# Gated attention's head norm: from TensorE sums and a ScalarE root to a GpSimd reduction and power

## What is computed

```python
y = xf * lax.rsqrt(jnp.mean(xf * xf, axis=-1, keepdims=True) + NORM_EPS)
return (y * g).astype(x.dtype)
```

## Time and profile before

| | |
|---|---|
| median of 3 runs | 1993.37 us (1993.0 to 1993.6) |
| the profiled execution | 1993.1 us, of which the span is 1991.3 us |
| granted TensorE clock | 0.999 of full speed |
| busy share of the span | PE 99%, PEld 83%, DVE 51%, ACT 35%, POOL 20% |
| dense tiles of this layer end, softmax steps begin | at about 152 us of the span |
| last transpose of the softmax steps | at 240.4 us |

### The profile page before, as it was taken

One profiled execution on the slowest core, in us unless ns is written; L12 is line 12 of the kernel. 1 busy time (PEld: TensorE's weight loads), 2 busy tenths in 40 slices (PEclk: granted clock), 3 DMA queues, 4 the chain that ended last, 5 costly groups with the idle time before them and its releaser, 6 DMA issues.

```text
span 1991.3 us, 27158 instructions
## 1 busy us (share of the span) xinstructions
PE 1975.5 (99%) x11044; PEld 1656.8 (83%) x11044; DVE 1019.7 (51%) x1391; ACT 694.5 (35%) x1008; POOL 404.9 (20%) x212
## 2 busy tenths in 40 slices
PE   9999999999999999999999999999999999999998
PEld 7878888888888888889888888888877888888887
DVE  5468758357345336626727535642543664322435
ACT  6357643122124323315312212534434252222222
POOL 1000007686600101000669661000000200000000
PEclk9999999999999999999999999999999999999999
DMA  6221134444333232232445442232221223323231
GB/s 198 74 61 44 46 114 159 157 139 153 123 104 117 84 97 85 85 113 89 148 140 167 148 146 87 85 106 76 70 80 64 86 84 106 102 99 106 84 106 64
DMA packets 135032, 208.91 MB, mean 105 GB/s; under 512 B 6346, under 2 KB 105864, under 8 KB 134920
## 3 DMA queue, kind: packets, MB, share of 16 engines
q1 hardware_dynamic: 125952, 180.37, 28.0%
q0 software_dynamic: 6912, 25.17, 3.8%
q10 hardware_dynamic: 2056, 1.76, 0.3%
HBM read 205.18 MB, written 2.10 MB: 104 GB/s over the span
## 4 chain that ended last, share of the span: by engine, by line
PE 94%; DVE 3%; ACT 2%; issue 0%; POOL 0%; ACTq 0%; POOLq 0%
PE ps L2149 28%; PE ps L2151 28%; PE ps L2150 28%; PE ps L2210 1%; PE ps L2600 1%; PE ps L2203 1%; PE ps L2202 1%; PE ps L2611 1%; PE ps L2700 1%; PE ps L2173 1%; PE ps L2792 1%; PE ps L2155 0%; DVE m L1460 0%; PE ps L2589 0%; PE ps L2588 0%
## 5 line engine op out<-in xcount | busy, mean ns | idle before, releaser
L1382 DVE TENSOR_TENSOR w_lo<-w_raw,w_hi 128x2048 fp32r<-128x2048 f32 x149 | 349.9, 2349 | 569.2 <-ACT w_hi L726 569.2
L2149 PE MATMUL ps<-x_hi,w_hi 128*128 128x512 f32 x1240 | 487.8, 393 | 0.4 <-DVE w_lo L1382 0.4
L2151 PE MATMUL ps<-x_hi,w_lo 128*128 128x512 f32 x1240 | 482.9, 389 | 0.0
L2150 PE MATMUL ps<-x_lo,w_hi 128*128 128x512 f32 x1240 | 482.8, 389 | 0.0
L726 ACT ACTIVATE w_hi<-w_raw 128x2048 fp32r<-128x2048 f32 x151 | 288.9, 1913 | 536.0 <-PE ps L2151 434.9
L2149 PEld LDWEIGHTS ps<-x_hi,w_hi 128*128 128x128 f32 x1240 | 233.3, 188 | 50.0 <-issue 2.5
L2151 PEld LDWEIGHTS ps<-x_hi,w_lo 128*128 128x128 f32 x1240 | 232.8, 188 | 49.1
L2150 PEld LDWEIGHTS ps<-x_lo,w_hi 128*128 128x128 f32 x1240 | 233.0, 188 | 46.3
L2149 PE MATMUL ps<-w_hi,h_hi 128*128 128x512 f32 x688 | 267.8, 389 | 0.0
L2151 PE MATMUL ps<-w_hi,h_lo 128*128 128x512 f32 x688 | 267.7, 389 | 0.0
L2150 PE MATMUL ps<-w_lo,h_hi 128*128 128x512 f32 x688 | 267.6, 389 | 0.0
(11 more groups left out here) (404 smaller groups left out, 2695.5 us busy)
## 6 DMA issues: line engine op xcount, KB each, us to landing
w_raw<-in_ffn_w SPq DMA_DIRECT2D x64, 1024.0 KB, 5.4
ada_w<-in_w_ada POOLq DMA_DIRECT2D x48, 512.0 KB, 4.1
w_raw<-in_w_ffn_in SPq DMA_DIRECT2D x22, 1024.0 KB, 5.1
w_raw<-in_w_in SPq DMA_DIRECT2D x20, 1024.0 KB, 5.4
w_raw<-in_o_w_in SPq DMA_DIRECT2D x16, 1024.0 KB, 5.4
w_raw<-in_w_ffn_out SPq DMA_DIRECT2D x11, 1024.0 KB, 4.9
w_raw<-in_e_w_in SPq DMA_DIRECT2D x9, 1024.0 KB, 5.4
w_raw<-in_o_w_out SPq DMA_DIRECT2D x8, 1024.0 KB, 4.8
```

Source lines behind the costliest of these rows:

```text
L1382: nc.vector.tensor_tensor(w_lo[:, slot, :], w_raw[:, slot, :], w_hi[:, slot, :].bitcast(F32), ALU.subtract).then_inc(w_lo_ready, 1)
L2149: nc.tensor.matmul(dst, a_hi, b_hi, start=start, stop=False)
L2150: nc.tensor.matmul(dst, a_hi, b_lo, start=False, stop=False)
L2151: return nc.tensor.matmul(dst, a_lo, b_hi, start=False, stop=stop_)
```

## The change

The sum over partitions is made by GpSimd with one `partition_all_reduce` over all four heads (128x2048), which leaves the sum on all partitions. GpSimd then scales it and adds the epsilon (TENSOR_SCALAR) and raises it to -0.5 (TENSOR_TENSOR with the operation pow) for each head. VectorE multiplies these into `o_gla` inside the softmax steps, at u = 3, 6, 8 and 10. The TensorE sums and spreads, ScalarE's root and VectorE's reciprocal go. The first copy of `n_prob_t` waits for the reduction, since it overwrites the squares. Two waits of TensorE on `gn_done` go with the PSUM banks that they protected.

```diff
+        gn_root = place("gn_root", [P, 4, SEQ], Y_ + 44)
...
+            pool.wait_ge(gn_sq, 1)
+            chain.link(nc.gpsimd.partition_all_reduce(gn_root[:, :, :].rearrange("p h t -> p (h t)"),
+                                                      gn_square[:, :, :].rearrange("p h t -> p (h t)"), P,
+                                                      bass.bass_isa.ReduceOp.add))
+            pool.sem_inc(gn_summed, 1)
+            for hd in range(GLA_HEADS):
+                part = gn_root[:, hd, :]
+                chain.link(nc.gpsimd.tensor_scalar(part, part, 4.0 / P, 4.0 * EPS, ALU.mult, ALU.add))
+                nc.gpsimd.tensor_tensor(part, part, neg_half[:, 0:1].broadcast_to([P, SEQ]), ALU.pow).then_inc(gn_rooted, 1)
...
-                if x == 18:
-                    act.wait_ge(gn_mm, 1)
-                    nc.scalar.activation(gn_sum[:, :], ps[:, 4, :], ACT.Sqrt, scale=4.0 / P,
-                                         bias=small[:, 21:22]).then_inc(gn_ms, 1)
...
             take_r(DENSE_E)
+            act.wait_ge(gn_summed, 1)
             for u in range(N_N):
...
             def gn_scale(hd):
-                dve.wait_ge(gn_spread, hd + 1)
-                nc.vector.scalar_tensor_tensor(o_gla[:, hd, :], o_gla[:, hd, :], gla_norm[:, hd:hd + 1], ps[:, 3 + hd, :],
+                dve.wait_ge(gn_rooted, hd + 1)
+                nc.vector.scalar_tensor_tensor(o_gla[:, hd, :], o_gla[:, hd, :], gla_norm[:, hd:hd + 1], gn_root[:, hd, :],
                                                ALU.mult, ALU.mult).then_inc(gn_done, 1)
...
-                    dve.wait_ge(gn_ms, 1)
-                    nc.vector.reciprocal(gn_sum[:, :], gn_sum[:, :]).then_inc(gn_rs, 1)
-                if x == 19:
-                    for hd in range(GLA_HEADS):
-                        gn_scale(hd)
...
+                if u in (3, 6, 8, 10):
+                    gn_scale((3, 6, 8, 10).index(u))
...
-                if x == 17:
-                    gn_sums()
...
-                if x == 19:
-                    gn_spreads()
...
                 if u >= 2:
                     pe.wait_ge(n_exped, 2 * u - 2)
-                elif u:
-                    pe.wait_ge(gn_done, 1)
-                else:
+                elif u == 0:
                     pe.wait_ge(bank_free, 4 + DENSE_E)
...
                 if u:
                     pe.wait_ge(n_copied, 2 * (u - 1) + z + 1)
-                else:
-                    pe.wait_ge(gn_done, 2 + 2 * z)
```

More of the change, by code:

```diff
@@ L304, in program @@
             "gla_a", "gla_am", "gla_ket", "gla_ds", "gla_s", "gla_o", "gla_oe"))
-        gn_sq, gn_mm, gn_ms, gn_rs, gn_spread, gn_done = (sem(x) for x in (
-            "gn_sq", "gn_mm", "gn_ms", "gn_rs", "gn_spread", "gn_done"))
+        gn_sq, gn_summed, gn_rooted, gn_done = (sem(x) for x in ("gn_sq", "gn_summed", "gn_rooted", "gn_done"))
         cmp_multiplied, cmp_copied = sem("cmp_multiplied"), sem("cmp_copied")
@@ L2525, in o_gla_of @@
                 o.then_inc(gla_o, 1)
[L2527 to L2538, removed]
             def in_the_middle(x):
```

## The result

The changed kernel takes 2299.2 us (median of 4 runs, 2298.33 to 2299.49) against 1993.4 us: the ratio is 1.153, 95% interval 1.1521 to 1.1548. The change costs 305.8 us. The range on record ended at 2033 us.

What follows compares the result with a forecast made beforehand. TensorE, 94% of the chain, was taken as the bound. Terms: -2.1 (matmuls) + 0.9 (reduction) + 11.9 (shared ports) + 1.4 (products) = +12.1 us on 1993.1, with 0.3 to the median 2005.5 us; range 1991 to 2033 us.

Steps and rivals of the forecast that it cites:

- The size of the power: GpSimd's power on 128x512, in no row: taken as 2.7 times a 1.4 us scaling, 4 us per head.
- The place of the loss: Forecast in the softmax steps: VectorE's scalings held at the shared ports while GpSimd runs its powers, +11.9 us.
- the rival of the slow routine: Powers beyond 7 us a head make GpSimd bound the first softmax steps: about 2015 us upward, chance 0.20.
- VectorE idle ahead of the new products: Sign in the softmax steps that the roots are late, and the ports not the cause; no size given.
- I assume that a long power holds the ports throughout: Softmax steps: each 4 us power blocks VectorE's scalings, so a step takes 6.3 us instead of 2.5.
- the +11.9 us: Softmax steps: port stalls beside GpSimd's scaling and power pairs, +0.5 for the first and +11.4 for the other three.
- The row of 1.67 us: Earlier one-column GpSimd power beside a long VectorE scaling: 1.67 instead of 0.60 us, ending 0.43 us after VectorE's.
- The reduction: GpSimd's sum beside VectorE's compressed attention chain: 12.3 us long, four instructions held 0.9 us each, +0.9 us.
- the rows at 454.00: VectorE beside an earlier reduction: a two-SBUF-tile instruction took 1.57 for 0.69 us, the cast behind it 1.29 for 0.43.
- What went: TensorE's sums and spreads of the old norm, 1.00 + 1.07 us: -2.1 us, the most the change can bring.
- the covered reciprocal: VectorE's reciprocal in the old norm, 3.35 us, hidden beside TensorE's other work; its removal counted at nothing.
- The late reduction: Rival: the reduction ends past 159.2 us and holds ScalarE's copies, 1.5 us at 24.5 us length; chance 0.03.

Runs made afterwards that it cites:

- without powers: The changed kernel with GpSimd's four powers left out, the root missing from the output: 2001.5 us, ratio 1.0041 to the kernel before.
- the moved reduction: The changed kernel with its four powers left out and the reduction started only after weight tile 10's low part: 1993.75 us, ratio 1.0004 to the kernel before.

## Why the prediction was wrong

**The size of the power** is the step that failed: "I take the ratio of the two one-column rows, 0.60 / 0.22 = 2.7, as that of the running part too". It measured 81.97 us where the step had 4, twenty times as much. The bounds held (1.28 and 195 us), but the choice between them did not rest on a row: the surplus of 0.38 us on one column was taken for start-up, and 0.16 of it was the price of the column. The row that is nearest in kind, the power itself, bounded from above and was the better guide; the product of the same shape shares only the shape. The range stopped at 12 us and left 0.12 beyond it, too little for a cost with two ends a factor 150 apart.

**The place of the loss** was named only in the rival of the slow routine: VectorE waits for the roots, the scalings stand behind it, TensorE behind these. Its arithmetic holds with the measured size: 155.8 + 4 x (1.4 + 82) puts the fourth root at 489.4 us, and its power ended at 489.0 (a start 0.6 us later and slightly shorter pairs nearly cancel). One of the prediction's own signs of being wrong, VectorE idle ahead of the new products, is what the profile shows. The memset of `v_cmp` is a point that all kernels share. Its line in GpSimd's timeline and the transposes of the steps, changed kernel first, then without powers:

```profile
92.98 0.53 POOL L645 MEMSET v_cmp<- 128x512 f32 x1 [75.13 <-PE ps L2431]
...
L2583 PEld LDWEIGHTS ps<-ident,n_prob x160: 137/141/231, 167.8 to 546.7; 128*128 128x128 f32 x160
```

```profile
93.95 0.53 POOL L645 MEMSET v_cmp<- 128x512 f32 x1 [75.16 <-PE ps L2431]
...
L2583 PEld LDWEIGHTS ps<-ident,n_prob x160: 137/140/143, 169.1 to 249.4; 128*128 128x128 f32 x160
```

Before, the memset is at 92.15 us and the transposes at 160.6 to 240.2. Counted from the memset to the last transpose, the changed kernel is 305.7 us longer: 6.4 us until the first transpose (7.2 of stall, less 2.1 of matmuls, and a remainder of 1.3, where the clock is low behind the stall), 0.7 us that the steps cost also without powers, 292.2 us of waits for the roots, and 6.4 us more in the steps (378.9 - 80.3 - 292.2). In that last part TensorE runs at the lower clock behind each wait, and two pairs of VectorE's scalings meet GpSimd's next scaling (1.70 us for 0.87, 1.82 for 1.00). It is a remainder, not an experiment.

**"I assume that a long power holds the ports throughout"** was wrong, and it was the whole mechanism of the +11.9 us. Powers leave the ports to VectorE in the changed kernel and beside the kernel before. The row of 1.67 us showed a power waiting for VectorE, which says nothing about the reverse.

**The reduction** was sized rightly in itself (12.3 us forecast, 11.89 measured) and wrongly in what it does to others: +0.9 us where 7.2 came, 8.5 with the remainder that goes with the clock. The step took 0.9 us per instruction from the rows at 454.00, which began 2.6 us before that reduction's end; in the changed kernel the product came 1.1 us after the reduction's start and stood until 146.86, 2.2 us before its end. How long an instruction stands depends on its kind, too. VectorE's timeline in the changed kernel, reduction from 137.20 to 149.09 us, has a second product of two SBUF tiles:

```profile
147.56 0.69 DVE L1591 TENSOR_TENSOR cmp_p<-cmp_p,cmp_one 128x512 f32<-128x512 f32 x1 [0.69 <-ACT cmp_p L979]
```

and with the moved reduction, from 146.99 to 158.88 us, the first unit's two scalings one by one:

```profile
155.17 1.23 DVE L1696 TENSOR_SCALAR n_prob<-n_prob,att_stat,branch_gate 128x512 f32<-128x512 f32 x1
```

```profile
156.31 2.85 DVE L1696 TENSOR_SCALAR n_prob<-n_prob,att_stat,branch_gate 128x512 f32<-128x512 f32 x1
```

The first product was let in when about three quarters of the reduction had passed (146.86 - 0.69 = 146.2 us), and so was the first scaling (155.17 + 1.23 - 0.5 = 155.9 us). What came after that point fared by its kind. The second product, of two SBUF tiles, was not held at all. The second scaling stood until 0.3 us behind the reduction's end, and so did the cast at 455.60, 1.29 us for 0.43. The nearest reading: both kinds are held for the first three quarters or so, and from then on only scalings and casts. The rows of before did not show the long part of it. The Trainium skill's lock for the whole instruction, set aside in the prediction, would have given some 9 us (the 0.9 and 8 more), close to what came.

**What went** was right as far as the traces tell: with the moved reduction the steps begin some 2.5 us earlier, 2.1 of it from TensorE's matmuls, which leaves at most 0.4 for the covered reciprocal and the rest. Nothing contradicts its role as the upper bound: no kernel of this study came more than 1.3 us under the one before, and none of those computes the norm. **The late reduction** did not occur: in the changed kernel it ended at 149.09 us, and ScalarE's first copy began at 168.60.

## What to carry to other kernels

A price known only on one column is two unknown numbers in one row: before such an operation goes onto wide tiles beside a tight stage, time it at two widths, and until then take the surplus as if it were paid for every column. First ask what the change can bring at most (here 2.1 us of 1993) and set that against the worst row-based price (4 x 195 us). And a row that shows A waiting for B does not show how long B would wait for A; look at where in the other's run it began, too.

## What the runs showed of the hardware that was not expected

- A power on GpSimd costs 0.40 us and 0.159 us per column, the same for 4 partitions as for 128 and for ones as for other values. A value per token is therefore cheap when tokens lie on partitions (four columns) and dear when they lie along the free dimension (four times 512).
- While a power runs (41 and 82 us), VectorE's scalings and its products of two SBUF tiles pass unhindered (0.74 and 1.22 us, as alone). Plain products hold the scalings (1.10 for 0.74 us). A reduction over partitions holds both for about its first three quarters (8.57 for 0.69); a scaling that comes after that still stands until it ends (2.85 for 0.5), a product of two SBUF tiles does not (0.69).
- Four sums over partitions onto 32 columns each take 1.00 us together, onto 128 columns each 3.59 us.
